# Low-rank products and head sums as rounded high and low parts, in a hybrid decoder block

## What is computed

```
w = -softplus(-(w0 + tanh(xw) @ w_up)) - 0.5      # xw: 64 columns
a = sigmoid(a0 + xa @ a_up)                       # xa: 64 columns
g = sigmoid(xg) @ g_up                            # xg: 160 columns
kk = k * k_k;  kk = kk / max(norm(kk over the 64 of a head), 1e-12)
k = k * (1 + (a - 1) * k_a)
bonus = sum(r * k * r_k over the 64 of a head) * v
```

## Time and profile before

| | |
|---|---|
| median of 3 runs | 1002.21 us (1001.06 to 1003.77) |
| the profiled execution | 1002.2 us, its span 1000.2 us |
| mean granted TensorE clock | 0.995 |
| TensorE busy | 963.4 us, 96% of the span |
| VectorE, ScalarE, GpSimd busy | 399.7, 424.7, 375.1 us |

### The profile page before, as it was taken

The page is one execution under the profiler, slowest core; times in us unless marked ns, Lnnn a source line. Parts: engine busy times, 40 slices in busy tenths (PEclk is TensorE's granted clock), DMA queues, the critical chain, the costliest instruction groups (busy, mean ns, idle before and its releaser), DMA issues.

```text
span 1000.2 us, 15861 instructions
## 1 busy us (share of the span) xinstructions
PE 963.4 (96%) x6791; PEld 796.0 (80%) x6791; DVE 399.7 (40%) x624; ACT 424.7 (42%) x665; POOL 375.1 (37%) x175
## 2 busy tenths in 40 slices
PE   6999999989999988999989999999999999999986
PEld 4885877777879988888868888888888888888865
DVE  4110258777564435137425343443434300101445
ACT  6244354344565335352336444444443421412546
POOL 2441443332224112334433344444444444344260
PEclk9999999999999989999999999999999999999999
DMA  8431433322111000224422333333333332324222
GB/s 256 105 101 43 105 86 83 85 85 65 43 49 39 5 3 3 64 86 135 138 85 64 101 89 106 89 101 100 90 106 87 103 121 90 102 88 126 74 74 85
DMA packets 115067, 86.45 MB, mean 86 GB/s; under 512 B 2821, under 2 KB 99991, under 8 KB 114999
## 3 DMA queue, kind: packets, MB, share of 16 engines
q1 hardware_dynamic: 114808, 85.37, 29.0%
q10 hardware_dynamic: 190, 0.08, 0.0%
HBM read 83.34 MB, written 2.10 MB: 85 GB/s over the span
## 4 chain that ended last, share of the span: by engine, by line
PE 73%; ACT 2%; POOL 2%; issue 1%; DVE 1%; POOLq 0%; DVEq 0%; ACTq 0%
PE bank L508 13%; PE bank L509 13%; PE bank L510 13%; PE bank L552 8%; PE bank L553 8%; PE bank L554 8%; PE bank L777 2%; PE bank L787 2%; PE bank L686 1%; PE bank L701 1%; PE bank L674 1%; PE bank L759 1%; PE bank L748 1%; PE bank L727 1%; POOL pleg_w_lo L488 1%
## 5 line engine op out<-in xcount | busy, mean ns | idle before, releaser
L488 POOL TENSOR_TENSOR w_lo<-raw,w_hi 128x1024 fp32r<-128x1024 f32 x138 | 333.1, 2414 | 530.6 <-ACT w_hi L1022 530.6
L1022 ACT ACTIVATE w_hi<-raw 128x1024 fp32r<-128x1024 f32 x138 | 146.4, 1061 | 364.5 <-issue 213.3
L508 PE MATMUL bank<-hT_hi,w_hi 128*128 128x512 f32 (+1 forms) x736 | 286.7, 390 | 2.0 <-POOL w_lo L488 1.9
L510 PE MATMUL bank<-hT_hi,w_lo 128*128 128x512 f32 (+1 forms) x736 | 283.2, 385 | 0.0
L509 PE MATMUL bank<-hT_lo,w_hi 128*128 128x512 f32 (+1 forms) x736 | 283.0, 385 | 0.0
L508 PEld LDWEIGHTS bank<-hT_hi,w_hi 128*128 128x128 f32 x736 | 138.3, 188 | 31.5 <-issue 2.1
L510 PEld LDWEIGHTS bank<-hT_hi,w_lo 128*128 128x128 f32 x736 | 138.2, 188 | 27.8
L509 PEld LDWEIGHTS bank<-hT_lo,w_hi 128*128 128x128 f32 x736 | 138.3, 188 | 27.3 <-issue 0.7
L1796 DVE SCALAR_TENSOR_TENSOR cbuf<-bank,params,cbuf 128x511 f32<-128x511 f32 x48 | 36.0, 750 | 133.9 <-ACT cbuf L1359 133.9
L552 PE MATMUL bank<-w_hi,g_hi 128*128 128x512 f32 x184 | 71.7, 389 | 0.0
L554 PE MATMUL bank<-w_hi,g_lo 128*128 128x512 f32 x184 | 71.6, 389 | 0.0
(11 more groups left out here) (258 smaller groups left out, 1304.9 us busy)
## 6 DMA issues: line engine op xcount, KB each, us to landing
raw<-in_w_up_dram SPq DMA_DIRECT2D x48, 512.0 KB, 3.8
raw<-in_w_in_dram SPq DMA_DIRECT2D x33, 512.0 KB, 4.0
raw<-in_w_down_dram SPq DMA_DIRECT2D x24, 512.0 KB, 3.7
raw<-in_w_gate_dram SPq DMA_DIRECT2D x16, 512.0 KB, 3.9
raw<-in_w_out_dram SPq DMA_DIRECT2D x8, 512.0 KB, 3.9
raw<-in_w_ple_gate_dram SPq DMA_DIRECT2D x8, 512.0 KB, 3.9
xs<-in_x_dram SPq DMA_DIRECT2D x4, 512.0 KB, 5.2
raw<-in_w_branch_a_dram SPq DMA_DIRECT2D x4, 512.0 KB, 3.4
```

The costliest lines, as they stand in the source:

```text
L488: nc.gpsimd.tensor_tensor(low(n)[:, :], raw[:, n % RAW_SLOTS, :], high(n)[:, :].bitcast(F32), ALU.subtract).then_inc(*step("pool", ("lo", n)))
L508: nc.tensor.matmul(o, wh, ah, start=first, stop=False)
L510: return nc.tensor.matmul(o, wl, ah, start=False, stop=last)
L1022: nc.scalar.activation(high(u)[:, :], raw[:, u % RAW_SLOTS, :], ACT.Copy) \
```

## The change

Both parts of the low-rank inputs and weights are formed, and the products become rounded ones, three for each fp32 one. The 32 leftover rows of `g_up` are stacked: high, low and high data (`lx_3`) against high, high and low weights (`lw_3`) in one matmul of 96 rows; two more transfers bring the copies of those rows. ScalarE casts the high parts behind the activations, GpSimd forms the low part of the weights ahead of the low part of unit rw 5, VectorE the low parts of the inputs behind shift 3. A head sum becomes two rounded products, of the high and of the low part of its data; ScalarE casts the high part, VectorE subtracts. `bonus_sum(p)` moves from behind `key_norm(p + 1)` to behind the unit before it. On VectorE c(p) moves ahead of b(p + 1).

```diff
@@ SyncE
-  sp.dma_start(lora_w[0:32, 2, :], ins["rw_g_up"][0, P:, :]).then_inc(lora_in, 16)
+  for r in (0, 32, 64):
+      sp.dma_start(lora_w[r:r + 32, 2, :], ins["rw_g_up"][0, P:, :]).then_inc(lora_in, 16)
@@ GpSimd, before the low part of unit n
+  if n == UIDX[("rw", 5)]:
+      gp.wait_ge(*done("act", "lora_hi"))
+      nc.gpsimd.tensor_tensor(lw_lo[:, :, :], lora_w[:, 0:2, :], lw_hi[:, :, :].bitcast(F32), ALU.subtract) \
+          .then_inc(*step("pool", ("lora_lo",)))
@@ TensorE, low-rank products
-  pe.wait_ge(lora_in, 64)
-  pe.wait_ge(*done("act", "lora_act"))
+  pe.wait_ge(*done("act", "lora_hi"))
+  pe.wait_ge(*done("dve", "lora_lo"))
+  pe.wait_ge(*done("pool", "lora_lo"))
   for i in range(NPAIR):
-      o = begin("lw", i)
-      nc.tensor.matmul(o[:, :], lora_w[0:64, 0, c], lora_x[0:64, 0, :], start=True, stop=True)
-      o = begin("la", i)
-      nc.tensor.matmul(o[:, :], lora_w[64:128, 0, c], lora_x[64:128, 0, :], start=True, stop=True)
+      ow, oa = begin("lw", i), begin("la", i)
+      for k, (w, x) in enumerate(((lw_hi, lx_hi), (lw_hi, lx_lo), (lw_lo, lx_hi))):
+          mm = nc.tensor.matmul(ow[:, :], w[0:64, 0, c], x[0:64, 0, :], start=k == 0, stop=k == 2)
...
+          mm = nc.tensor.matmul(oa[:, :], w[64:128, 0, c], x[64:128, 0, :], start=k == 0, stop=k == 2)
       o = begin("lg", i)
-      nc.tensor.matmul(o[:, :], lora_w[:, 1, c], lora_x[:, 1, :], start=True, stop=False)
-      nc.tensor.matmul(o[:, :], lora_w[0:32, 2, c], lora_x[0:32, 2, :], start=False, stop=True)
+      split3(o[:, :], lw_hi[:, 1, c], lw_lo[:, 1, c], lx_hi[:, 1, :], lx_lo[:, 1, :], True, False)
+      nc.tensor.matmul(o[:, :], lw_3[0:96, c], lx_3[0:96, :], start=False, stop=True)
@@ TensorE, head sums
-      nc.tensor.matmul(o[:, :], cst("heads"), src, start=True, stop=True)
+      pe.wait_ge(*done("act", "sum_hi", tag, p))
+      nc.tensor.matmul(o[:, :], heads_r[:, :], sum_hi[:, p % 2, :], start=True, stop=False)
+      pe.wait_ge(*done("dve", "sum_lo", tag, p))
+      nc.tensor.matmul(o[:, :], heads_r[:, :], sum_lo[:, p % 2, :], start=False, stop=True)
@@ TensorE, behind unit qk i
+  if i % 3 == 1 and i // 3 >= 1:
+      bonus_sum(i // 3 - 1)
   if i % 3 == 2:
       key_norm(i // 3)
-      if i // 3 >= 1:
-          bonus_sum(i // 3 - 1)
@@ ScalarE, behind the activations of lora_x
+  act.wait_ge(*previous("act"))
+  nc.scalar.activation(lx_hi[:, :, :], lora_x[:, 0:2, :], ACT.Copy)
+  for r in (0, 64):
+      nc.scalar.activation(lx_3[r:r + 32, :], lora_x[0:32, 2, :], ACT.Copy)
+  act.wait_ge(lora_in, 16 * 6)
+  nc.scalar.activation(lw_hi[:, :, :], lora_w[:, 0:2, :], ACT.Copy)
+  nc.scalar.activation(lw_3[0:96, :], lora_w[0:96, 2, :], ACT.Copy).then_inc(*step("act", ("lora_hi",)))
+  act.wait_ge(cst_in, 16)
+  nc.scalar.activation(heads_r[:, :], cst("heads"), ACT.Copy)
@@ ScalarE, head sums
+  def summed_hi(tag, p):
+      if tag == "kn":
+          act.wait_ge(*previous("act"))
+          if p >= 2:
+              act.wait_ge(*done("pe", "bn", p - 2))
+      else:
+          act.wait_ge(*done("dve", "rk", p))
+          act.wait_ge(*done("pe", "kn", p))
+      nc.scalar.activation(sum_hi[:, p % 2, :], Sc[:, p % 2, :], ACT.Copy)
...
   if i % 3 == 0:
       squares(i // 3)              # now ends with summed_hi("kn", i // 3)
+      if i // 3:
+          summed_hi("bn", i // 3 - 1)
@@ ScalarE, v0 units
       before(("v0", s))
+      if s == 1:
+          summed_hi("bn", NPAIR - 1)
@@ VectorE, shifts (after 13, 14, 0, 1, 2, 3)
+  dve.wait_ge(*done("act", "lx_hi", 64))
+  V.tensor_tensor(lx_lo[:, :, :], lora_x[:, 0:2, :], lx_hi[:, :, :].bitcast(F32), ALU.subtract)
+  V.tensor_tensor(lx_3[32:64, :], lora_x[0:32, 2, :], lx_3[0:32, :].bitcast(F32), ALU.subtract)
+  dve.wait_ge(*done("act", "lora_hi"))
+  V.tensor_tensor(lw_3[64:96, :], lora_w[64:96, 2, :], lw_3[64:96, :].bitcast(F32), ALU.subtract)
@@ VectorE, pairs
   pre_a(0)
-  for p in range(NPAIR):
-      if p + 1 < NPAIR:
-          pre_a(p + 1)
-      pre_b(p)
-      if p:
-          pre_c(p - 1)
+  summed_lo("kn", 0)
+  pre_a(1)
+  pre_b(0)
+  for p in range(NPAIR - 1):
+      summed_lo("bn", p)
+      if p + 2 < NPAIR:
+          pre_a(p + 2)
+      summed_lo("kn", p + 1)
+      pre_c(p)
+      pre_b(p + 1)
+  summed_lo("bn", NPAIR - 1)
   pre_c(NPAIR - 1)
```

More of the change, by code:

```diff
@@ L102 @@
     "act_E", "act_U", "act_U1", "act_Vt", "act_Am", "act_Wp", "act_chain", "act_exp", "act_g_hi",
-    "act_gate", "act_gelu", "act_graw", "act_gn_sd", "act_hi", "act_kk_sq", "act_kn", "act_la", "act_lg", "act_lora_act",
+    "act_gate", "act_gelu", "act_graw", "act_gn_sd", "act_hi", "act_kk_sq", "act_kn", "act_la", "act_lg", "act_lora_hi", "act_lx_hi", "act_sum_hi", "dve_lora_lo", "dve_sum_lo", "pool_lora_lo",
     "act_lw", "act_mg_hi", "act_own", "act_pg", "act_pp", "act_psum_read", "act_pt", "act_qk", "act_rms", "act_sq",
@@ L263, in build @@
         lora_w = at("lora_w", 118, [P, 3, RW])
+        lx_hi, lx_lo = [at(n, kb, [P, 2, SEQ], F32R) for n, kb in (("lx_hi", 56), ("lx_lo", 60))]
+        lw_hi, lw_lo = [at(n, kb, [P, 2, RW], F32R) for n, kb in (("lw_hi", 64), ("lw_lo", 68))]
+        lx_3, lw_3 = at("lx_3", 72, [P, SEQ], F32R), at("lw_3", 74, [P, RW], F32R)
+        sum_hi, sum_lo = [at(n, kb, [P, 2, SEQ], F32R) for n, kb in (("sum_hi", 101), ("sum_lo", 105))]
+        heads_r = at("heads_r", 109, [P, P], F32R)
         Lt, Et, Ei, Sc = [at(n, 112 + 4 * i, [P, 2, SEQ]) for i, n in enumerate(("Lt", "Et", "Ei", "Sc"))]
@@ L611, in _ @@
             pe.wait_ge(cst_in, 16)
-            pe.wait_ge(lora_in, 64)
-            pe.wait_ge(*done("act", "lora_act"))
+            pe.wait_ge(*done("act", "lora_hi"))
+            pe.wait_ge(*done("dve", "lora_lo"))
+            pe.wait_ge(*done("pool", "lora_lo"))
             for i in range(NPAIR):
                 c = slice(i * P, (i + 1) * P)
-                o = begin("lw", i)
-                nc.tensor.matmul(o[:, :], lora_w[0:64, 0, c], lora_x[0:64, 0, :], start=True, stop=True) \
-                    .then_inc(*step("pe", ("lw", i)))
-                o = begin("la", i)
-                nc.tensor.matmul(o[:, :], lora_w[64:128, 0, c], lora_x[64:128, 0, :], start=True, stop=True) \
-                    .then_inc(*step("pe", ("la", i)))
+                ow, oa = begin("lw", i), begin("la", i)
+                for k, (w, x) in enumerate(((lw_hi, lx_hi), (lw_hi, lx_lo), (lw_lo, lx_hi))):
+                    mm = nc.tensor.matmul(ow[:, :], w[0:64, 0, c], x[0:64, 0, :], start=k == 0, stop=k == 2)
+                    if k == 2:
+                        mm.then_inc(*step("pe", ("lw", i)))
+                    mm = nc.tensor.matmul(oa[:, :], w[64:128, 0, c], x[64:128, 0, :], start=k == 0, stop=k == 2)
+                mm.then_inc(*step("pe", ("la", i)))
                 o = begin("lg", i)
-                nc.tensor.matmul(o[:, :], lora_w[:, 1, c], lora_x[:, 1, :], start=True, stop=False)
-                nc.tensor.matmul(o[:, :], lora_w[0:32, 2, c], lora_x[0:32, 2, :], start=False, stop=True) \
+                split3(o[:, :], lw_hi[:, 1, c], lw_lo[:, 1, c], lx_hi[:, 1, :], lx_lo[:, 1, :], True, False)
+                nc.tensor.matmul(o[:, :], lw_3[0:96, c], lx_3[0:96, :], start=False, stop=True) \
                     .then_inc(*step("pe", ("lg", i)))
@@ L627, in _, with head_sums @@
                 feature_unit(("rw", i), "rw", i)
-            def head_sums(tag, src, p):
+            def head_sums(tag, p):
+                pe.wait_ge(*done("act", "sum_hi", tag, p))
                 o = begin(tag, p)
-                nc.tensor.matmul(o[:, :], cst("heads"), src, start=True, stop=True).then_inc(*step("pe", (tag, p)))
+                nc.tensor.matmul(o[:, :], heads_r[:, :], sum_hi[:, p % 2, :], start=True, stop=False)
+                pe.wait_ge(*done("dve", "sum_lo", tag, p))
+                nc.tensor.matmul(o[:, :], heads_r[:, :], sum_lo[:, p % 2, :], start=False, stop=True) \
+                    .then_inc(*step("pe", (tag, p)))
             def key_norm(p):
-                pe.wait_ge(*done("act", "kk_sq", p))
-                head_sums("kn", Sc[:, p % 2, :], p)
+                head_sums("kn", p)
             def bonus_sum(p):
-                pe.wait_ge(*done("dve", "rk", p))
-                head_sums("bn", Sc[:, p % 2, :], p)
+                head_sums("bn", p)
             parts = [0]
@@ L1090, in _ @@
             nc.scalar.activation(lora_x[:, 1, :], lora_x[:, 1, :], ACT.Sigmoid).then_inc(*step("act"))
-            nc.scalar.activation(lora_x[0:32, 2, :], lora_x[0:32, 2, :], ACT.Sigmoid).then_inc(*step("act", ("lora_act",)))
+            nc.scalar.activation(lora_x[0:32, 2, :], lora_x[0:32, 2, :], ACT.Sigmoid).then_inc(*step("act"))
+            act.wait_ge(*previous("act"))
+            nc.scalar.activation(lx_hi[:, :, :], lora_x[:, 0:2, :], ACT.Copy).then_inc(*step("act"))
+            for r in (0, 64):
+                nc.scalar.activation(lx_3[r:r + 32, :], lora_x[0:32, 2, :], ACT.Copy).then_inc(*step("act", ("lx_hi", r)))
```

(24 more changed lines are left out.)

## The result

The changed kernel took 1008.43 us, median of 4 runs (1007.12 to 1009.93); the kernel before, on the same chip, 1001.82 (1001.06 to 1003.77). The ratio is 1.0057, interval [1.0039, 1.0074]: slower by 6.6 us between the medians, where +7.8 was forecast.

What follows compares the result with a forecast made beforehand. The prediction took TensorE to bound the kernel: queue terms +4.0 − 4.0 − 3.3 − 2.5 + 8.8 = +3.0, plus 4.8 for its clock, on 1002.2 gave 1010.0 us, range 1001 to 1016.

Steps and rivals of the forecast that it cites:

- The stop in front of rw 5: TensorE waits once before unit rw 5, as new casts and a subtraction delay its low part; +4.0 us.
- Low-rank products: Four pairs on TensorE shrink from 12.75 to 8.8 us as rounded matmuls with three exposed loads each; −4.0 us.
- the bound with exposed loads: Low-rank products with loads exposed at all six 64-row matmuls and no pair together: 15.5 us, +2.7.
- Head sums: Eight fp32 sums on TensorE become two rounded matmuls each, 0.45 instead of 0.86 us; −3.3 us.
- The two old stops: TensorE's late restarts at 171.39 and 191.00 vanish because VectorE's new order frees the decay buffers sooner; −2.5 us.
- Three bonus stops: TensorE waits behind qk 4, 7 and 10 for bonus-sum parts, with VectorE and GpSimd colliding; about 2.9 each, +8.8 us.
- The clock: TensorE's clock falls behind two of the four new stops, at 2.4 us each; +4.8 us.
- The sum: All queue terms on TensorE, +3.0 us, plus 4.8 for the clock, added to 1002.2: 1010.0 us.
- Rival 1: TensorE's stops cost what the queues say and its clock never falls; 1005.2 us, chance 0.18.
- rival 3: Weight loads are exposed in every 64-row low-rank product on TensorE; 6.7 us more, 1016.7 us, chance 0.07.
- rival 4: The stop before rw 5 doesn't come because the casts overlap more than counted; 1003.6 us, chance 0.10.
- Rival 2: The bonus chain on VectorE escapes the collision and row groups hide their loads; 996.8 us, chance 0.13.

Runs made afterwards that it cites:

- e2: Changed kernel with the low-rank setup casts and subtractions spread over later units on ScalarE, GpSimd and VectorE; 1001.17 us.
- e8: Kernel before with only the low-rank products split, setup spread as in e2, fp32 head sums and old orders; 997.0 us.
- e6: e7 with VectorE running the next pair's chain (b) ahead of this pair's last step (c), as in the kernel before; 1002.42 us.
- e5: Changed kernel with GpSimd forming only 128 of 1024 columns of the low parts of units qk 5, 8 and 11; 1005.05 us.
- e1: Changed kernel with TensorE taking a pair's bonus sum behind the next pair's key sum again; 1003.85 us.
- e4: Changed kernel with only GpSimd's subtraction of the low-rank weights moved one unit later, to unit rw 6; 1006.51 us.
- e3: Changed kernel with the edits of e1 and e2 together; 995.29 us.
- e7: e3 with the key sum's low part ahead of the bonus sum's on VectorE; 997.3 us.
- e9: e7 with ScalarE forming the bonus sum's high part one unit later and VectorE's scan ahead of its low part; 996.48 us.

## Why the prediction came out as it did

- **The stop in front of rw 5, +4.0: right.** 4.16 by TensorE's matmuls, 7.3 with the clock behind it (e2). The working held in its parts: the high part starts at 59.12 (59.6 forecast), GpSimd's subtraction takes 2.36 (2.40), the low part ends near 64 (64.3).
- **Low-rank products, −4.0: right in kind, 0.7 too small.** The 0.2 for a load at a change of row groups was right, but it was charged at three places of a pair and is paid at two: the step from 128 to 96 rows costs nothing. Over four pairs that is the 0.7. The two 64-row products of a pair still start together (83.08 and 83.09), so the bound with exposed loads is excluded. e8 confirms the term by time, −4.7.
- **Head sums, −3.3: right by the trace,** 0.45 a sum (129.17 to 129.62) against 0.86. No run has this part by itself.
- **The two old stops, −2.5: right.** Neither wait is in the changed kernel's list, nor ScalarE's wait for the decay buffers in its timeline; e6, with the old order, has that wait of ScalarE again, and e8, with it too, both old stops of TensorE (1.0 and 1.2).
- **Three bonus stops, +8.8: right,** 2.9 each, and by the mechanism that was forecast: the product at 142.09 in a time base some 1.5 later than before's, the collision at the TENSOR_TENSOR where the prediction had moved it, and in all four pairs (L1590 takes 2.31 to 2.64, median 2.54), then high and low part one after the other. e5 takes the collision away; pair 0's stop shrinks to 1.0, where 0.9 had been given for no collision, pair 2's to 1.2, and pair 1's only to 2.7. What the prediction didn't see is what these stops covered: with the sum back in its place only 4.6 of the 8.8 and of the clock return (e1), and the key sum's low part is late by 3.3. The new order on VectorE was costed at −2.5 and nothing against it; its wait was hidden only by the bonus stops.
- **The clock, +4.8 for two of four stops: 1.1 too small, 5.9 measured.** Both the count and the price differ: it fell behind three of four, at 2.8, 1.6 and 1.5 instead of 2.4 each. That the fall goes with the stop is shown by e2 (no stop, no fall there); one of 2.8 is enough for it in e4. For the shorter ones the runs show no rule, so taking two of four was a guess that came near.
- **The sum** came to +7.8 and the spans differ by 7.9, but that close a match is luck. Gained beyond the forecast were 0.7 at the products, 0.7 ahead of rw 5, 0.2 at the old stops and 0.4 of small differences; lost beyond it 1.1 at the clock, 0.2 at the first stop and 0.8 in the rest. By the medians the change is +6.6, 1.2 less than forecast. Rival 1 (the clock never falls) is refuted by the windows, rival 3 (loads exposed) by the products' timeline, rival 4 (no first stop) by the wait of 4.0. Rival 2 needed the collision to vanish; in the traces of the changed kernel, e3, e7 and e9 pair 0's multiplication takes 2.64 or 2.65 each time, and in e5, where it doesn't, later collisions remain.

**What stays open.** No kernel reached 989 to 991, the sum with all three savings and no new wait. Each order of VectorE and ScalarE that was tried left 3.3 us or more of stops at the head sums or at a unit's low part. The traces show a common reason that the prediction didn't count. TensorE's own round for a pair is three units and two sums, 76 x 0.227 = 17.2 us. VectorE's, from one bonus product to the next, is longer in the first two rounds of every kernel with c ahead of b: 21.8 and 21.7 in the changed kernel, 20.0 and 20.0 in e5, 19.4 and 20.5 in e3, 21.6 and 19.4 in e7, 21.1 and 21.0 in e9. In the changed kernel three instructions of each of these rounds are stretched by GpSimd to 2.3 to 2.5, some 6 us together (estimated from their lengths elsewhere, 0.46, 0.17 and 0.69). Without them the round would fit into TensorE's; with them TensorE must stop somewhere, and the order only chooses where. No run takes all of them away, so this is argued from the traces. Whether an order without a stop exists isn't settled. Nor is what decides whether a stop of about 2 us lowers the clock.

## What to carry to other kernels

Splitting an fp32 product in three rounded ones paid for itself where TensorE is the bound, but the casts and subtractions that it needs go into in-order queues that feed the very same engine: put them where each queue has cover, a piece at a time (7.3 us here, more than the products saved). A consumer moved ahead by one unit (5.4 us) wants a producer chain that is shorter by as much, less the cover that it had; count the chain with the collision in it, as it follows the phase. And a stop can hide another: before a wait is removed, ask what came ready during it, and whether the producer's whole round, and not only its last chain, is shorter than the consumer's (here 20 us against 17).

## What the runs showed of the hardware

- **The clock behind short stops.** Stops of 4.0 (the changed kernel, e1, e5), 3.3 and 2.3 (e6), 2.87 (e7) and 2.8 (e4) lowered it, each followed by some 3 to 7 us at the lower level. With a wait of 2.15 and, one matmul later, 0.23 it fell behind two of three in the changed kernel and behind one of three in e2 and e4. A wait of 1.86 lowered it in e3 (granted 0.50 from 162 to 164), one of 1.88 in e1 and one of 1.92 with 0.22 behind it in e5 did, and one of 1.86 in e9 didn't; nor did one of 2.25 at 506.58 in the kernel before. In the stretch where two weight-low-part waits of 0.99 and 1.24 stood it stayed up. So lengths alone, near 2 us, don't tell.
- **VectorE beside GpSimd.** A 0.69 us instruction of VectorE took 2.3 to 2.9 where GpSimd's low part had started up to 0.8 before it (136.75 beside 136.45; 149.64 beside 149.00 in e5; 154.73 beside 154.04 in e9), also one with a single tensor input (2.54 at 144.53 beside GpSimd's 3.01 at 143.78; 0.46 at 123.68 with none beside it). By the Trainium skill ("SBUF — State Buffer", the part on the shared pair of ports) whichever starts first keeps the pair for its whole instruction; these rows agree (the multiplication at 136.75 ends at 139.39, 0.5 behind GpSimd's end at 138.85).
- **Weight loads.** In rounded fp32 the loads were hidden behind the matmul ahead of them in the same row group too (starts 0.23 apart for full-height matmuls, 0.24 from 83.42 to 83.66 at 64 rows), and 0.2 was exposed at the step from 64 to 128 rows and at that from 96 to 64, none from 128 to 96. The Trainium skill ("TensorE: Matmul & The Clock Gate", The mechanism) has loads overlap only where the row groups differ; here it is rather the other way round, and the measurement decides.
